# Delta-rule heads: norm and transpose of a token tile one tile later with two buffers, two scalings on ScalarE, waits and filler steps moved

## The reference, cut to what matters

```python
kb = kc * bc
a_mat = jnp.where(strict, jnp.einsum('nbhtd,nbhsd->nbhts', kb, kc) * gam, 0.0)
rhs = jnp.concatenate([vc * bc, kb * jnp.exp(G)[..., None]], axis=-1)
sol = lax.linalg.triangular_solve(a_mat + eye, rhs, left_side=True, lower=True, unit_diagonal=True)
u0, w = sol[..., :dv], sol[..., dv:]
attn = jnp.einsum('nbhtd,nbhsd->nbhts', qc, kc) * gam
kg = kc * jnp.exp(G[..., -1:] - G)[..., None]
def step(S, inp):
    u = u0_c - jnp.einsum('bhtd,bhdv->bhtv', w_c, S)
    o = jnp.einsum('bhtd,bhdv->bhtv', qg_c, S) + jnp.einsum('bhts,bhsv->bhtv', at_c, u)
    S = gl_c[..., None, None] * S + jnp.einsum('bhsd,bhsv->bhdv', kg_c, u)
```

## Time and profile before

| what | value |
|---|---|
| median of 3 runs | 1769.35 us (1767.39 to 1771.38) |
| the profiled execution's own time | 1769.78 us |
| its span | 1768.0 us |
| PE busy | 1608.0 us, 91% of the span |
| DVE busy | 975.3 us, 55% |
| ACT busy | 607.0 us, 34% |
| mean granted PE clock | 0.953 of full speed |

### The profile page before, as it was taken

One profiled execution on the slowest core, in us unless ns is written; L12 is line 12 of the kernel. 1 busy time (PEld: TensorE's weight loads), 2 busy tenths in 40 slices (PEclk: granted clock), 3 DMA queues, 4 the chain that ended last, 5 costly groups with the idle time before them and its releaser, 6 DMA issues. The chain is left out here.

```text
span 1768.0 us, 31295 instructions
## 1 busy us (share of the span) xinstructions
PE 1608.0 (91%) x11168; PEld 1454.0 (82%) x11168; DVE 975.3 (55%) x2118; ACT 607.0 (34%) x1411; POOL 181.7 (10%) x384
## 2 busy tenths in 40 slices
PE   6999999995999999798889998999999999978798
PEld 2789898985999999798779987878878888866798
DVE  1665565563665765525465553767557657653622
ACT  2523232321222232424543432344443443432421
POOL 1000000000000000001000000112312312311000
PEclk8999999997999999899889898999999999998899
DMA  9434252505243332324313231211111111010223
GB/s 304 109 104 114 72 150 63 144 6 117 63 131 90 89 107 71 86 82 133 77 32 78 77 80 31 75 41 51 40 40 50 40 40 50 5 66 1 83 84 108
DMA packets 195255, 140.85 MB, mean 80 GB/s; under 512 B 18332, under 2 KB 178584, under 8 KB 194916
## 3 DMA queue, kind: packets, MB, share of 16 engines
q1 hardware_dynamic: 177772, 130.16, 25.8%
q10 hardware_dynamic: 17400, 9.60, 1.9%
HBM read 128.58 MB, written 11.15 MB: 79 GB/s over the span
## 5 line engine op out<-in xcount | busy, mean ns | idle before, releaser
L166 PE MATMUL bank<-hT,w_high 128*128 128x288 f32 x1152 | 367.8, 319 | 25.4 <-ACT retention_qkT_raw L1162 9.6
L167 PE MATMUL bank<-hT,w_low 128*128 128x288 f32 x1152 | 348.2, 302 | 0.0
L168 PE MATMUL bank<-hT,w_high 128*128 128x288 f32 x1152 | 347.6, 302 | 0.0
L166 PEld LDWEIGHTS bank<-hT,w_high 128*128 128x128 f32 x1152 | 225.1, 195 | 39.4 <-issue 10.5
L167 PEld LDWEIGHTS bank<-hT,w_low 128*128 128x128 f32 x1152 | 225.5, 196 | 0.0
L168 PEld LDWEIGHTS bank<-hT,w_high 128*128 128x128 f32 x1152 | 224.9, 195 | 0.0
L166 PE MATMUL bank<-output_w_split,gT_high 128*128 128x256 f32 x512 | 145.1, 283 | 3.5 <-DVE gT_low L2433 3.5
L168 PE MATMUL bank<-output_w_split,gT_high 128*128 128x256 f32 x512 | 144.5, 282 | 0.0
L167 PE MATMUL bank<-output_w_split,gT_low 128*128 128x256 f32 x512 | 143.8, 281 | 0.0
L166 PEld LDWEIGHTS bank<-output_w_split,gT_high 128*128 128x128 f32 x512 | 97.3, 190 | 3.9 <-DVE gT_low L2433 3.7
L167 PEld LDWEIGHTS bank<-output_w_split,gT_low 128*128 128x128 f32 x512 | 97.9, 191 | 0.0
(11 more groups left out here) (456 smaller groups left out, 3615.7 us busy)
## 6 DMA issues: line engine op xcount, KB each, us to landing
x<-in_w_in_even SPq DMA_DIRECT2D x72, 512.0 KB, 5.0
x<-in_w_in_odd SPq DMA_DIRECT2D x56, 512.0 KB, 4.4
x<-in_w_ada SPq DMA_DIRECT2D x32, 256.0 KB, 4.3
front_w_ada<-in_w_ada SPq DMA_DIRECT2D x6, 1024.0 KB, 14.9
output_w_raw<-in_w_out_even SPq DMA_DIRECT2D x12, 512.0 KB, 3.4
output_w_raw<-in_w_out_odd SPq DMA_DIRECT2D x12, 512.0 KB, 3.5
gdn_E<-G_rows SPq DMA_DIRECT2D x8, 576.0 KB, 4.8
gT<-in_w_ada SPq DMA_DIRECT2D x16, 256.0 KB, 4.4
```

The source lines that it names most:

```text
L166: pe.matmul(out, w[0], x[1], start=first, stop=False)
L167: pe.matmul(out, w[1], x[0], start=False, stop=False)
L168: return pe.matmul(out, w[0], x[0], start=False, stop=last)
```

## The change

- The norm of tile t moves into the DVE program of tile t + 1 (behind that tile's o and behind its piece of other work), and the take-over of its transpose into tile t + 2; both of the last tiles' follow behind the loop. o and `sm` get two buffers each, used in turn; g keeps one.
- On PE `turn_g(t)` moves from the end of tile t + 1 to tile t + 2, right behind u and ahead of the filler steps. That of tile 3 stands in the next head's program, behind the transposes of tokens 0 to 3.
- ACT's copy of o_a no longer waits for the norm of the tile before, but for o of two tiles before.
- The scalings `kg` and `bv` leave DVE; ACT does each as five activations with a scale that is a column of its own for each partition: kg in level 0, bv in level 1.
- The transpose of X^T no longer waits for the prompt's attention; the wait stands ahead of the first Z batch. `XT1_ready` is given one instruction later (behind L1928).
- The wait for X^T ahead of w is split: tiles 0 and 1 wait for one half, 2 and 3 for the other, the sample for its own.
- Filler steps: 5 to 25 (was 23) ahead of the transposes of k and q, then 25 to 29, 29 to 36. The wait for `gT_copied` of the last head moves behind steps 5 to 25. In level 2, step 51 moves from behind ZZ to behind YY.

The diff, without the declarations and without the renaming of `o` and `sm` to two buffers on ACT and POOL:

```diff
...
     TB = (4, 6, 2, 3, 5)
-    LEVEL_FILL = ((38, 39, 40, 42, 43, 45), (45, 46, 47, 48, 49, 50), (50, 50, 51, 52, 52))
+    LEVEL_FILL = ((38, 39, 40, 42, 43, 45), (45, 46, 47, 48, 49, 50), (50, 50, 51, 51, 52))

...
                 turn_tokens(t)
+            if previous is not None:
+                turn_g(pe, previous, T - 2)
             project(pe, ahead, 0, 5)
...

-            pe.wait_ge(*s["tok_copied"].done(h, 1))
+            project(pe, ahead, 5, 25)
             pe.wait_ge(*s["gT_copied"].before(h, 0))
-            project(pe, ahead, 5, 23)
             pe.wait_ge(*s["tok_copied"].done(h, T - 1))
...
             last.then_inc(s["kq_psum"].sem, 1)
-            project(pe, ahead, 23, 27)
+            project(pe, ahead, 25, 29)
             pe.wait_ge(*s["kq_copied"].done(h, 0))
...
             last.then_inc(s["kk_psum"].sem, 1)
-            project(pe, ahead, 27, 36)
+            project(pe, ahead, 29, 36)
             pe.wait_ge(*s["XT1_ready"].done(h, 0))
-            pe.wait_ge(*s["attn_ready"].done(h, 0))
             pe.sem_inc(M.passed, 1)
...
                     pe.wait_ge(*s["N_copied"].done(h, 2 * n + i))
+                    if n == 0 and i == 0:
+                        pe.wait_ge(*s["attn_ready"].done(h, 0))
                     for t in group(i):
...
                     project(pe, ahead, fill[4], fill[5])
-            pe.wait_ge(*s["XT_ready"].done(h, 2 * NL - 1))
-            pe.wait_ge(*s["sample_XT"].done(h, 0))
             pe.wait_ge(*s["kv_scaled"].done(h, 0))
...
                 R = rows(t)
+                if t % 2 == 0 and t < PT:
+                    pe.wait_ge(*s["XT_ready"].done(h, 2 * (NL - 1) + t // 2))
+                if t == PT:
+                    pe.wait_ge(*s["sample_XT"].done(h, 0))
                 out = PS[2][:, t * P:t * P + R] if t < PT else PS[5][:, 0:DEC]
...
                 pe.wait_ge(*s["u_copied"].before(h, t))
+                if t == 0:
+                    pe.wait_ge(*s["bv_scaled"].done(h, 0))
                 pairs = [(tiles(XT, t), bv[0:R, t, :])] + ([(wN[:, cols(t)], S[:])] if t else [])
...
                 matmul_chain(pe, PS[6][0:R, 0:P], pairs).then_inc(s["u_psum"].sem, 1)
+                if t >= 2:
+                    turn_g(pe, h, t - 2)
                 project(pe, ahead, *((52, 55), (55, 58), (58, 60), (60, 61), (61, 62))[t])
...
                 pe.wait_ge(*s["u_copied"].done(h, t))
+                if t == 0:
+                    pe.wait_ge(*s["kg_scaled"].done(h, 0))
                 pe.sem_inc(M.passed, 1)
...
                     project(pe, ahead, 62, 64)
-                if t:
-                    turn_g(pe, h, t - 1)

...
                     take_projection(act, ahead, 4)
+                    act.wait_ge(*s["scale_b"].done(h, 0))
+                    for t in range(T):
+                        R = rows(t)
+                        last = act.activation(kg[0:R, t, :], tk[0:R, t, 1, :], ACT.Copy, scale=sc[0:R, 3, t:t + 1])
+                    last.then_inc(s["kg_scaled"].sem, 1)
                 elif n == 1:
...
                     take_projection(act, ahead, 5)
+                    for t in range(T):
+                        R = rows(t)
+                        last = act.activation(bv[0:R, t, :], tk[0:R, t, 2, :], ACT.Copy, scale=M["gcols"][0:R, 2, t, bass.ds(h, 1)])
+                    last.then_inc(s["bv_scaled"].sem, 1)
                 else:
...
                 act.wait_ge(*s["o_psum"].done(h, t))
-                act.wait_ge(*s["g_ready"].before(h, t))
-                act.activation(o_a[0:R, :], PS[7][0:R, P:2 * P], ACT.Copy).then_inc(s["o_copied"].sem, 1)
+                if t == 0:
+                    act.wait_ge(*s["g_ready"].before(h, 0))
+                elif t >= 2:
+                    act.wait_ge(*s["o_ready"].done(h, t - 2))
+                act.activation((o_a if t else o[0])[0:R, :], PS[7][0:R, P:2 * P], ACT.Copy).then_inc(s["o_copied"].sem, 1)
                 act.wait_ge(*(s["o_ready"].done(h, t - 1) if t else s["o_copied"].done(h, t)))
-                act.activation(sqj[0:R, :], (o if t else o_a)[0:R, :], ACT.Square, accum_out=sm[0:R, 0:1]).then_inc(s["squared"].sem, 1)
+                act.activation(sqj[0:R, :], o[t % 2][0:R, :], ACT.Square, accum_out=sm[0:R, t % 2, 0:1]).then_inc(s["squared"].sem, 1)
                 if t == 0:
...

+            def norm(t):
+                R = rows(t)
+                dve.wait_ge(*s["rstd_ready"].done(h, t))
+                dve.wait_ge(*s["gT_psum"].before(h, t))
+                dve.tensor_scalar(g[0:R, :], o[t % 2][0:R, :], sm[0:R, t % 2, 2:3], None, ALU.mult).then_inc(s["g_ready"].sem, 1)
+
+            def take_g(t):
+                dve.wait_ge(*s["gT_psum"].done(h, t))
+                dve.scalar_tensor_tensor(M["gT"][:, bass.ds(h + 8, 1), cols(t)].rearrange("p a t -> p (a t)"), gT_bank(t),
+                                         M["vec"][:, bass.ds(h + 56, 1)], zs[:, cols(t)], ALU.mult, ALU.mult
+                                         ).then_inc(s["gT_copied"].sem, 1)
+
             dve.wait_ge(*s["tok_squared"].done(h, 0))
...
             dve.wait_ge(*s["kv_scaled"].before(h, 0))
+            dve.wait_ge(*s["kg_scaled"].before(h, 0))
             dve.tensor_scalar(sc[:, 0, :], rn[:, :, 1], 0.5, None, ALU.mult)
...
             dve.tensor_tensor(blocks(XT[:, 0:SEQ]), each_block(M.c("ident")), blocks(Q[:, 0:SEQ]), ALU.subtract)
-            dve.tensor_tensor(tiles(XT, PT), M.c("ident", DEC, DEC), tiles(Q, PT), ALU.subtract).then_inc(s["XT1_ready"].sem, 1)
-            dve.tensor_tensor(atT[0:DEC, SEQ:TOK], PS[5][0:DEC, DEC:2 * DEC], E[0:DEC, 0, SEQ:TOK], ALU.mult)
+            dve.tensor_tensor(tiles(XT, PT), M.c("ident", DEC, DEC), tiles(Q, PT), ALU.subtract)
+            dve.tensor_tensor(atT[0:DEC, SEQ:TOK], PS[5][0:DEC, DEC:2 * DEC], E[0:DEC, 0, SEQ:TOK], ALU.mult).then_inc(s["XT1_ready"].sem, 1)
             dve.tensor_tensor(atT[:, 0:SEQ], PS[3][:, :], E[:, 0, 0:SEQ], ALU.mult).then_inc(s["attn_ready"].sem, 1)
...
             dve.wait_ge(*s["scale_b"].done(h, 0))
-            dve.tensor_tensor(kbe[:], tk[:, :, 1, :], spread(sc[:, 2, :]), ALU.mult)
-            dve.tensor_tensor(kg[:], tk[:, :, 1, :], spread(sc[:, 3, :]), ALU.mult)
-            dve.tensor_tensor(bv[:], tk[:, :, 2, :], spread(gcol(2)), ALU.mult).then_inc(s["kv_scaled"].sem, 1)
+            dve.tensor_tensor(kbe[:], tk[:, :, 1, :], spread(sc[:, 2, :]), ALU.mult).then_inc(s["kv_scaled"].sem, 1)

...
                 if t:
-                    dve.wait_ge(*s["g_ready"].before(h, t))
-                    dve.scalar_tensor_tensor(o[0:R, :], PS[7][0:R, 0:P], M["gcols"][0:R, 0, t, bass.ds(h, 1)], o_a[0:R, :],
+                    if t >= 2:
+                        dve.wait_ge(*s["g_ready"].done(h, t - 2))
+                    dve.scalar_tensor_tensor(o[t % 2][0:R, :], PS[7][0:R, 0:P], M["gcols"][0:R, 0, t, bass.ds(h, 1)], o_a[0:R, :],
                                              ALU.mult, ALU.add).then_inc(s["o_ready"].sem, 1)
-
                 if t == 0:
...
                     silu_conv(dve, ahead, 2)
-                dve.wait_ge(*s["rstd_ready"].done(h, t))
-                dve.wait_ge(*s["gT_psum"].before(h, t))
-                dve.tensor_scalar(g[0:R, :], (o if t else o_a)[0:R, :], sm[0:R, 2:3], None, ALU.mult).then_inc(s["g_ready"].sem, 1)
-                for tt in ([t - 1] if t else []) + ([t] if t == T - 1 else []):
-                    dve.wait_ge(*s["gT_psum"].done(h, tt))
-                    dve.scalar_tensor_tensor(M["gT"][:, bass.ds(h + 8, 1), cols(tt)].rearrange("p a t -> p (a t)"), gT_bank(tt),
-                                             M["vec"][:, bass.ds(h + 56, 1)], zs[:, cols(tt)], ALU.mult, ALU.mult
-                                             ).then_inc(s["gT_copied"].sem, 1)
+                if t:
+                    norm(t - 1)
+                if t >= 2:
+                    take_g(t - 2)
+            norm(T - 1)
+            take_g(T - 2)
+            take_g(T - 1)

...
                 pe_turn(pe, H - 1, None, H - 2)
+                turn_g(pe, H - 1, T - 2)
                 turn_g(pe, H - 1, T - 1)
...
                 pe.wait_ge(*s["cache_saved"].before(H, 0))
```

More of the change, by code:

```diff
@@ L1504, in gdn_heads @@
         ML = sb("A_level", [P, 2, TOK])
-        u, o_a, o, g, sqj = (place[:, 4 * D + i * P:4 * D + (i + 1) * P] for i in range(5))
+        u, o_a, o_even, o_odd, g, sqj = (place[:, 4 * D + i * P:4 * D + (i + 1) * P] for i in range(6))
+        o = (o_even, o_odd)
         zr, tz = (x[:].rearrange("p t d -> p (t d)")[:, 0:TOK] for x in (kn, qn))
         zs = sb("z_silu", [P, TOK])
-        sm = sb("small", [P, 4])
+        sm = sb("small", [P, 2, 4])
         St = [M["gates"][:, 0, i * P:(i + 1) * P] for i in range(2)]
@@ L1521, in gdn_heads @@
                  "N_psum": 2 * NL, "N_copied": 2 * NL, "Z_psum": 2 * NL, "Z_copied": 2 * NL, "ZZ_psum": 2 * NL, "Y_ready": 2 * NL,
```

(6 more changed lines are left out.)

## The result

| | before | changed |
|---|---|---|
| median of 10 runs | 1767.06 us (1763.31 to 1771.38) | 1762.90 us (1755.53 to 1765.92) |
| ratio, 95% interval | | 0.9970 (0.9957 to 0.9983) |
| span of the profiled execution | 1768.0 us | 1762.9 us |

The change makes the kernel 0.3% faster. The forecast was +0.07%, so its sign is wrong, and 1762.9 lies just under the stated range. Some 2 us of that distance are the footing: the median of before is 1767.06 over ten runs, where three gave 1769.35. The rest is the change itself, and it is in the size of terms, as the next rows show: two of them, the gain upstream and the loss in the tile loop, were each wrong by 0.4 us a head.

The account below looks back on a forecast made before the run. PE, in written order, was bound by its work plus a few waits on DVE, ACT or POOL chains. Six heads at 2.2 - 1.8 = +0.4 us, head 6 0, head 7 -1.2: +1.2, giving 1770.6 us; range 1764 to 1777.

Parts of the forecast that it names:

- the gain upstream: From a head's start up to w: 1.8 us a head gained, bounds 1.3 to 2.0.
- the loss in the tile loop: From w to the next head's tokens: PE stalls at transposes of g, losing 2.2 us a head, bounds 1.3 to 2.8.
- YY moves by 1.47 us: Level 0: two scalings leaving DVE bring Y, and so PE's YY, 1.47 us earlier; bounds 1.2 to 1.5.
- then 0.15: Tile loop: after each stall, the transpose of g itself holds PE for 0.15 us.
- X^T (0.59 forecast): Upstream: transposes of X^T, released by L1928, start 0.59 us earlier; this is contained in YY's shift.
- Level 2: Filler step behind YY and split wait: w starts 0.35 us earlier, bounds 0 and 0.5.
- ACT's scalings: Five bv scalings take 1.5 us and fit ACT's 1.49 us idle in level 1; kg fits level 0; cost nothing.
- Rival C: ACT's bv scalings outlast their cover by 0.8 us, holding up level 2 by 0.4 a head; 1773 us, chance 0.06.
- Rival B: Tile loop: same stalls but 0.31 us for each transpose, upstream at 1.5; net loss 1.2 a head, 1775.5 us, chance 0.22.
- Heads 6 and 7: Last two heads: head 6, without `low`, unchanged; head 7, without filler or other work, gains 1.2 us.
- rival A: Tile loop: transposes of g ready when PE comes; 2.4 us a head gained, 1751 us; chance 0.18 including its half-way case.
- rival A's half-way case: Tile loop: only tile 2's stall stays, the loop loses 1.2 us a head; 1764 us, chance 0.11.

Follow-up runs that it names:

- The cut in two: Two kernels: the change without its tile loop (ratio 0.9917, middle head 2.22 us shorter); the tile loop alone on the kernel before (1.0061, 1.84 us longer).
- The fourth experiment: Changed kernel with norm and take-over of g moved ahead of DVE's other work (save_cache, low, SiLU): 1751.3 us, ratio 0.9898, middle head 63.04 us.
- one moved line: Changed kernel with PE's transpose of g moved from right behind the u matmul to behind both matmuls with u: 1744.03 us, ratio 0.9858.
- one half alone: All of the change except its tile loop, on the kernel before: 1754.3 us against 1769.83, ratio 0.9917.

## Why the prediction was wrong, by its own steps

**The steps that failed are two terms that nearly cancel.** Upstream was forecast to gain 1.8 us a head (1.3 to 2.0), the loop to lose 2.2 (1.3 to 2.8). The cut in two measures 2.22 and 1.84. Both errors are 0.4 us, both on the same side, and times six that is 5 us: nearly all of the distance behind the footing. The loop lay inside its bounds, upstream outside. In both the mechanism came as described, and a piece was mis-sized: upstream mostly "YY moves by 1.47 us", in the loop "then 0.15" for each transpose.

**Y and YY (1.47 forecast, 1.65 measured in a middle head).** The text held that DVE's Y still comes last, so that YY moves by what the two scalings took, with 0.3 us of wait left. Y moved by 1.86 us: the two scalings, and 0.44 more because the copies fell into a pause of POOL's. So PE itself is the last, with no wait left, and YY moves by what PE can: the 1.10 us that its wait cost and the 0.55 us by which X^T came earlier. The forecast held this last gain to be contained in that of YY; with the scalings beside it, it adds to it. The bound "1.5" left out that another instruction of the chain could change its own length. In head 0, the head of the forecast's rows, YY moved from 20.39 to 18.80 us behind the scales, 1.59.

**X^T (0.59 forecast):** 0.55 in the middle heads, where the two filler steps ahead of the transposes of k and q cost nothing. In head 0 these ran over by 0.14 us, just above the "0.0 to 0.1" given, and X^T moved from 1146.57 - 1134.67 = 11.90 us behind the scales to 11.49: 0.41.

**Level 2 (0.35 forecast, 0 to 0.5):** w starts 0.35 us earlier, as forecast. What the text put at nothing, without naming it, is that a batch that starts out of a wait takes longer than one that doesn't: to the next batch YY takes 1.74 us instead of 1.86, and w 1.35 instead of 1.45. The sum of the four, 1.65 + 0.12 + 0.35 + 0.10, is the 2.22 measured.

**ACT's scalings:** the cover held. In the changed kernel five of bv take 1.56 us and X's copy follows without a gap:

```profile
1227.16 1.56 ACT L1861 ACTIVATE gdn_v_beta<-gdn_qkv_tokens,gcols 128x128 f32<-128x128 f32 x5
1228.76 0.82 ACT L1868 ACTIVATE gdn_X_and_XT<-bank 128x256 f32<-128x256 f32 x2
```

Taken was 1.5, and no PE wait follows. Rival C has fallen. The Trainium skill's price ("ScalarE: Activation LUTs", section "What ACT_TABLE_LOAD costs") gave an estimate of 1.56 for five, which the row meets to the digit.

**The tile loop (2.2 forecast, 1.84 measured): the stalls right, the transposes too dear.** Each stall came where it was put and as long, counted from start to start: 1.40 us at tile 2 (1.4 forecast), released by the norm, 1.15 at tile 3 (1.2), released by the take-over, and 0.18 at tile 4 (0.2). Each state matmul came earlier than the text had it: behind w by 9.64, 13.02 and 16.01 us, forecast 9.8, 13.3 and 16.4. The largest piece is the 0.15 us for each transpose, read from five of them in 0.80 us: alone between a wait and the filler it costs 0.06, three times, so 0.27 in all. Another 0.1 is w's own length, which is already counted upstream. Rival B's dearer transposes (0.31) were wrong by more. The fourth experiment shows that the norm stands still behind `low` and the SiLU on DVE. That agrees with the strict order that the Trainium skill, "TensorE: Matmul & The Clock Gate", section "Architectural detail: the array is 16× 32×32, not 1× 128×128", states for VectorE.

**Heads 6 and 7.** Head 6 was forecast at no change and takes 0.33 us less (61.61 instead of 61.94). The last head was forecast at -1.2; from its scales to its last take-over of g it went from 56.37 to 54.32, so -2.05. Of that, -1.43 lies ahead of w (1.1 forecast) and -0.62 in the loop (0.1 forecast), where without filler the chain is DVE's and the norm leaves it: DVE waited 1.49 us for POOL ahead of most norms in before. The -1.43 is near the forecast partly by luck. The granted clock rises from 0.50 to 1.00 of full speed (1.2 to 2.4 GHz) within level 0 of this head, while PE works without a pause, and it rose earlier in the changed kernel: there the ZZ batch took 1.61 us, in before 2.31. In turn the second product of k and q took 2.34 instead of 1.90, so that X^T gained only 0.13 of the 0.59 forecast. These shifts of the clock, and not the change, make 0.4 us of the 1.43.

**What it means for the chances.** 0.50 was put on "the same" and 0.32 on slower. With a net of 0.4 us a head from terms of 2 us whose bounds were 0.7 and 1.5 us wide, the sign was hardly known: the bounds of the two terms reach from -0.7 to +1.5 a head, and a net of -0.4 lies inside. The 0.18 for faster hung on rival A's mechanism alone; it should have held the lower part of the forecast's own bounds as well. That rival A's half-way case, 1764, lies next to the measured 1762.9 is chance: its mechanism, an absent stall in tile 3, did not occur.

## What to carry to other kernels

A move that takes an engine's wait away must be followed through every queue it passes: here it freed DVE of POOL and then made PE wait for DVE, ahead of the matmul that everything else needs. Put a transfer that nobody needs soon behind the link of the chain, not ahead of it: one moved line took the kernel from 0.9970 to 0.9858 of the time before (each against its own run of before), some 1.1%. And where a change joins a gain and a loss, time the halves; their difference says nothing on either. Here one half alone was better than the whole (0.9917), and the whole with one line moved better still.

## What the runs showed of the hardware

Three copies of 128 x 3 on DVE take 0.378 us each beside POOL's tensor operations and 0.160 us with POOL idle; from the first to the next instruction that is 0.97 against 0.52 us. A scaling of 128 x 640 on DVE took 0.82 us when it started ahead of POOL's burst and 1.03 us when it started behind it (medians of eight heads, before and the kernel with the X^T edit). The Trainium skill, "SBUF — State Buffer", section "Who interferes with whom", says that a VectorE copy in a two-port mode and a GpSimd instruction lock each other out of a shared pair of ports for a whole instruction. The slow copies agree with it in kind; no row shows in which mode they ran. The runs show that it can cost 0.45 us of a 65 us head through three of the smallest instructions.

On PE, ten matmuls of 128 x 128 in f32 take 0.1 us longer when they start out of a wait (1.86 against 1.74 us for YY and its filler step, 1.45 against 1.35 for w), and a transpose that stands alone between a wait and the filler holds PE for 0.06 us, while five in a row take 0.80.
